# Sums of squares of the head norms as two fp32r matmuls on a split, in place of one fp32 matmul

## The reference, cut to what matters

```
mu = jnp.mean(o, axis=-1, keepdims=True)
var = jnp.mean(jnp.square(o - mu), axis=-1, keepdims=True)
o = (o - mu) * lax.rsqrt(var + EPS)
```

```
o = _rms_norm(o, o_g.astype(f32).reshape(HG_HEADS, HG_DV)).reshape(bsz, seq, HG_WIDTH)
o = o * jax.nn.silu(g_raw.astype(f32))
```

## Time and profile before

| | us |
|---|---|
| median of 3 runs | 3059.87 |
| lowest, highest | 3058.55, 3060.05 |
| the profiled execution's own time | 3058.55 |
| span of its trace | 3056.8 |
| PE busy in the span | 3021.0 (99%) |
| POOL, DVE, ACT busy | 1411.2, 1692.7, 1133.5 |

### The profile page before, as it was taken

The page is one execution under the profiler, slowest core; times in us unless marked ns, Lnnn a source line. Parts: engine busy times, 40 slices in busy tenths (PEclk is TensorE's granted clock), DMA queues, the critical chain, the costliest instruction groups (busy, mean ns, idle before and its releaser), DMA issues.

```text
span 3056.8 us, 41047 instructions
## 1 busy us (share of the span) xinstructions
PE 3021.0 (99%) x13900; PEld 2395.4 (78%) x13900; DVE 1692.7 (55%) x2591; ACT 1133.5 (37%) x1713; POOL 1411.2 (46%) x1040
## 2 busy tenths in 40 slices
PE   8999999999999999999999999999999999999998
PEld 6877777877888887777777788877888888788886
DVE  7974575675434597576577644267772253621214
ACT  4233332364332423233245524236563333422223
POOL 5443443455455453443444555443434444454544
PEclk9999999999999999999999999999999999999999
DMA  4222212212232332222221132221213323232222
GB/s 148 97 69 69 96 69 82 84 42 83 97 102 95 128 99 72 92 75 66 79 90 56 36 131 96 96 97 63 77 68 98 103 83 103 83 103 97 96 96 90
DMA packets 73269, 267.86 MB, mean 88 GB/s; under 512 B 8128, under 2 KB 9024, under 8 KB 72768
## 3 DMA queue, kind: packets, MB, share of 16 engines
q1 hardware_dynamic: 70560, 254.84, 24.9%
q10 hardware_dynamic: 2592, 11.46, 1.0%
HBM read 262.07 MB, written 4.19 MB: 87 GB/s over the span
## 4 chain that ended last, share of the span: by engine, by line
PE 82%; issue 7%; POOL 5%; DVE 3%; DVEq 1%; ACT 0%; POOLq 0%; ACTq 0%
PE gem L356 18%; PE gem L358 18%; PE gem L357 18%; POOL wlo L290 5%; PE xp L500 4%; PE gem L744 2%; PE xp L489 2%; PE gem L746 2%; PE gem L745 2%; PE gem L476 2%; PE gem L477 2%; PE gem L475 2%; PE gem L587 2%; PE gem L610 1%; PE xp L646 1%
## 5 line engine op out<-in xcount | busy, mean ns | idle before, releaser
L290 POOL TENSOR_TENSOR wlo<-raw,whi 128x512 fp32r<-128x512 f32 x956 | 1315.7, 1398 | 1581.2 <-ACT whi L905 1580.9
L905 ACT ACTIVATE whi<-raw 128x1024 fp32r<-128x1024 f32 x478 | 504.6, 1056 | 675.8 <-PE gem L358 466.9
L356 PE MATMUL gem<-zhi,whi 128*128 128x512 f32 x1680 | 666.5, 397 | 0.3 <-DVE zlo L1503 0.3
L358 PE MATMUL gem<-zhi,wlo 128*128 128x512 f32 x1680 | 654.1, 389 | 0.0
L357 PE MATMUL gem<-zlo,whi 128*128 128x512 f32 x1680 | 653.7, 389 | 0.0
L356 PE MATMUL gem<-hhi,whi 128*128 128x512 f32 x1296 | 515.7, 398 | 0.0
L358 PE MATMUL gem<-hhi,wlo 128*128 128x512 f32 x1296 | 504.5, 389 | 0.0
L357 PE MATMUL gem<-hlo,whi 128*128 128x512 f32 x1296 | 504.3, 389 | 0.0
L356 PEld LDWEIGHTS gem<-zhi,whi 128*128 128x128 f32 x1680 | 315.5, 188 | 71.7 <-issue 7.0
L357 PEld LDWEIGHTS gem<-zlo,whi 128*128 128x128 f32 x1680 | 315.5, 188 | 70.7 <-issue 6.5
L358 PEld LDWEIGHTS gem<-zhi,wlo 128*128 128x128 f32 x1680 | 315.4, 188 | 66.0
(11 more groups left out here) (320 smaller groups left out, 3960.3 us busy)
## 6 DMA issues: line engine op xcount, KB each, us to landing
raw<-in_slabs SPq DMA_DIRECT2D x478, 512.0 KB, 3.4
U<-in_x SPq DMA_DIRECT2D x4, 512.0 KB, 7.8
U<-in_x ACTq DMA_DIRECT2D x1, 2048.0 KB, 8.6
xsave<-U ACTq DMA_DIRECT2D x1, 2048.0 KB, 6.5
U<-xsave ACTq DMA_DIRECT2D x1, 2048.0 KB, 8.9
out_y<-yr SPq DMA_DIRECT2D x8, 256.0 KB, 2.1
tab<-in_tab_ret ACTq DMA_DIRECT2D x2, 512.0 KB, 8.1
tab<-in_tab_att ACTq DMA_DIRECT2D x2, 512.0 KB, 3.6
```

The lines of the kernel that those rows point to most:

```text
L290: part = pool.tensor_tensor(wlo[:, k % 4, c], raw[:, k % 2, c], whi[:, k % 4, c].bitcast(f32), O.subtract)
L356: pe.matmul(o, wh, hi, start=(n == 0), stop=False)
L358: mm = pe.matmul(o, wl, hi, start=False, stop=(n == len(terms) - 1))
L905: act.activation(whi[:, k % 4, :], raw[:, k % 2, :], A.Copy).then_inc(hi_done, 1)
```

## The change

The sum over partitions was one fp32 matmul of the squares by fp32 ones. It becomes two fp32r matmuls into the same bank, of the high half and of the low half of the squares, by ones in fp32r. The halves are put into tile 7 of the pair that is free at that time (`zhi`/`zlo` of the layer; in the gating heads the names `Z[DEPTH][0]` on ACT and `zhi` on DVE are the buffer that the order below calls `hhi`). In retention heads DVE makes both halves behind its last add. In gating heads ACT makes the high half behind the square (a third 128x512 instruction, signal `hg_osh`), and DVE makes the low half in `square_rest`, behind the first level of `k_levels`, and signals `hg_osq`. The sum stands three rows later in heads 1 to 6 (25 and 23 for 22 and 20), two rows later in head 0 (29 for 27), and where it was in head 7 (23). ACT makes the fp32r ones once, at the start, and PE's first instruction waits for them too.

```diff
@@ tensor engine @@
             pe.wait_ge(consts, 1)
+            pe.wait_ge(ones_ready, 1)
...
                 def var(hd):
                     pe.wait_ge(ossq, L * 4 + hd + 1)
-                    pe.matmul(xp[:, 1, :], ones[:, :], TT[:, 2, :], start=True, stop=True).then_inc(ovar, 1)
+                    pe.matmul(xp[:, 1, :], ones_r[:, :], zhi[:, 7, :], start=True, stop=False)
+                    pe.matmul(xp[:, 1, :], ones_r[:, :], zlo[:, 7, :], start=False, stop=True)\
+                        .then_inc(ovar, 1)
...
                 pe.wait_ge(hg_osq, p + 1)
-                pe.matmul(xp[:, 2, :], ones[:, :], OSQ, start=True, stop=True).then_inc(hg_var, 1)
+                pe.matmul(xp[:, 2, :], ones_r[:, :], zhi[:, 7, :], start=True, stop=False)
+                pe.matmul(xp[:, 2, :], ones_r[:, :], zlo[:, 7, :], start=False, stop=True).then_inc(hg_var, 1)
                 rows(cuts[4], 32)
 
-            head_products(0, BLOCK_G + 1, BLOCK_U + 1, (14, 16, 18, 23, 27))
-            head_products(1, BLOCK_G + 2, BLOCK_U + 2, (0, 9, 13, 17, 22))
+            head_products(0, BLOCK_G + 1, BLOCK_U + 1, (14, 16, 18, 23, 29))
+            head_products(1, BLOCK_G + 2, BLOCK_U + 2, (0, 9, 13, 17, 25))
             with pe.Fori(2, 7) as p:
-                head_products(p, BLOCK_G + 1 + p, BLOCK_U + 1 + p, (0, 6, 11, 15, 20))
+                head_products(p, BLOCK_G + 1 + p, BLOCK_U + 1 + p, (0, 6, 11, 15, 23))
@@ scalar engine @@
             log_exp()
+            act.wait_ge(consts, 1)
+            act.activation(ones_r[:, :], ones[:, :], A.Copy).then_inc(ones_ready, 1)
             high(0, 0, False)
...
-                act.activation(OSQ, OH, A.Square).then_inc(hg_osq, 1)
+                act.activation(OSQ, OH, A.Square)
+                act.drain()
+                act.activation(Z[DEPTH][0][:, 7, :], OSQ, A.Copy).then_inc(hg_osh, 1)
                 act.wait_ge(hg_var, p + 1)
@@ vector engine @@
-                    tt(TT[:, 2, :], TT[:, 2, :], TT[:, 3, :], O.add).then_inc(ossq, 1)
+                    tt(TT[:, 2, :], TT[:, 2, :], TT[:, 3, :], O.add)
+                    dve.drain()
+                    dve.tensor_copy(zhi[:, 7, :], TT[:, 2, :])
+                    dve.drain()
+                    tt(zlo[:, 7, :], TT[:, 2, :], zhi[:, 7, :].bitcast(f32), O.subtract).then_inc(ossq, 1)
...
                     last = longer(KES[2 * w], KES[w], KF[w])
+                    if w == 16 and p is not None:
+                        square_rest(p)
...
+            def square_rest(p):
+
+                dve.wait_ge(hg_osh, p + 1)
+                tt(zlo[:, 7, :], OSQ, zhi[:, 7, :].bitcast(f32), O.subtract).then_inc(hg_osq, 1)
...
             update(7)
+            square_rest(7)
             head_end(7)
```

More of the change, by code:

```diff
@@ L96, in build @@
         ident = sb("ident", [P, P])
+        ones_r = sb("ones_r", [P, P], f32r)
         ones = sb("ones", [P, P])
@@ L241, in build @@
         hg_osq, hg_var, hg_rstd = sem("hg_osq"), sem("hg_var"), sem("hg_rstd")
+        hg_osh, ones_ready = sem("hg_osh"), sem("ones_ready")
         merged_in, merged_hi = sem("merged_in"), sem("merged_hi")
@@ L2083, in longer, with k_levels @@
                           factor[:, :, None].to_broadcast([P, n, T // n]), O.mult)
-            def k_levels():
+            def k_levels(p=None):
                 dve.tensor_copy(DEC[16], chunks(EB)[:, :, CHUNK16 - 1])
@@ L2157, in _ @@
                 el_k(hd)
-                k_levels()
+                k_levels(p)
                 head_end(p)
```

## The result

The changed kernel takes 3063.46 us (median of 20 runs) where the kernel before takes 3059.61 (20 runs): a ratio of 1.0013 with a 95% interval of 1.0007 to 1.0019. It is slower by 3.9 us. That is within my bound for no change (0.2%, 6.1 us) and within my range, but its sign is clear, and the forecast was +0.3 us: 3.6 us of what happened are not in my sum. One of the changed kernel's 20 runs took 7871 us, a slow one that the ratio leaves out; the others lie between 3062.30 and 3064.80.

The account below looks back on a forecast made before the run. PE was taken to bound the kernel, busy for 3021.0 of 3056.8 us. The terms -3.2 + 0.2 + 0.9 + 1.6 + 1.1 - 0.3 = +0.3 us gave a forecast of 3060.2 us, range 3056.0 to 3063.5.

Parts of the forecast that it names:

- The price of a matmul: At the 16 sums: fp32 matmul 0.85 us, fp32r pair 0.46, saving 0.395 each, at most 6.3 us.
- The retention heads: In the eight retention heads the added DVE work fits into slack, so all savings come through: -3.2 us.
- The start: At kernel start ACT makes the ones before its first copies and shifts all that follows: +0.2 us.
- The place in the gating heads: The later sum delays ACT's root, DVE's chain and the next scores; waits at the scores 7.5 us in all.
- the queue of 7.7 us: Behind the gating root, POOL's four and DVE's five instructions still take 7.7 us, with DVE now going first.
- Rival 1: In gating heads the chain behind the root doesn't hold PE, so the whole saving comes: 3053.8 us; chance 10%.
- its half: No wait at the scores in gating heads 2 to 6 alone, 3.0 us better: 3057.1 us; chance 9%.
- Rival 2: In gating heads POOL delays the low half and PE waits at the sum: up to +8.8 us, 3069; chance 5%.
- rival 3: At the sums, fp32r by a block of ones costs what fp32 did, saving missing: 3066.5 us; chance 4%.
- The step that failed is the sum's last one: Adding the terms for start, retention heads and gating heads over the whole kernel to +0.3 us.
- what a wait leaves behind it: In gating heads 2 to 6 PE waits 0.6 us each and comes out 0.21 later: +1.1 us in all.
- Head 0: In gating head 0 the pair waits 0.05 us and the scores of head 1 come later: +0.9 us.

Follow-up runs that it names:

- run 1: Kernel before with only the retention heads' part and the fp32r ones, gating heads unchanged: 3056.35 us against 3059.72.
- run 3: Kernel before, fp32 matmul kept, only the gating sums moved to 29, 25 and 23 rows from 27, 22 and 20: 3068.75 us against 3059.72.
- run 4: Changed kernel with the gating sums put back to 27, 22 and 20 rows: 3065.48 us against 3059.72 for the kernel before.
- run 5: Changed kernel with the gating sums one row earlier, at 28, 24 and 22 rows: 3060.45 us against 3059.37 for the kernel before.
- run 10: Changed kernel with the sums of gating heads 0 and 1 one row earlier (28 and 24): 3061.49 us against 3059.77 for the kernel before.
- run 12: Changed kernel with nothing altered, profiled a third time to see TensorE's clock: 3062.92 us.
- run 8: Kernel before with nothing altered, profiled once more to see TensorE's clock: 3061.26 us.
- run 2: Kernel before with only the gating heads' part of the change, retention heads unchanged: 3066.28 us against 3059.72.

## Why the prediction was wrong, point by point

The change in the changed kernel's trace, from the same marks in both traces (after minus before, us):

| stretch | forecast | measured |
|---|---|---|
| start | +0.2 | +0.1 |
| 8 retention heads | -3.2 | -3.4 |
| clock, 2040 to 2100 us | 0 | +0.7 |
| gating head 0 up to the scores of head 1 | +0.9 | +1.5 |
| clock behind these scores | 0 | +1.4 |
| head 1 | +1.6 | +1.6 |
| heads 2 to 7 | +0.8 | +1.8 |
| sum | +0.3 | +3.7 |

**The price of a matmul** was right: 0.85 us for the fp32 one, and 0.46 for the pair, so that a retention head is 108.17 us long for 108.59. **The retention heads** were right in sign and size, and run 1 alone gives -3.4 us.

**The start** was right: the first matmul stands at 11.05 us for 10.83, and by row 6 the difference is 0.1.

**The place in the gating heads** was right as a mechanism. The places of the root (0.66 behind the pair for 0.65 forecast), of `head_end` (2.19 for 2.08 behind the pair) and the queue of 7.7 us are those of the working, the waits at the scores are 7.0 us (7.5 forecast): 2.5 in head 1, 1.9 in head 2 (2.0 forecast) and 0.5 in the others (0.6). Run 3 shows that the place alone costs 9.0 us, and run 4 that the pair can't stand at the old one, though one of the three rows can be given back (run 5). Rival 1 is out with its half, as are rivals 2 and 3: PE hardly waits at the sum, and the pair is cheap. (Rival 2's 8.8 us count POOL's full 1.25 us in each of 7 heads; with the slack of 0.6 us that it names, 0.65 and 4.6 us are left.) One reading was wrong: DVE was to go first in the queue, and POOL went first in all seven heads, as before (2295.29, and DVE's L1513 at 2295.33).

**The step that failed is the sum's last one:** "-3.2 + 0.2 + 0.9 + 1.6 + 1.1 - 0.3 = +0.3 us". It put TensorE's clock at nothing, took a wait at its own length, and had head 0 at 0.9 where 1.5 was measured. Of the 3.4 us between the forecast and the trace, 2.1 are the clock (1.4 of them behind the new waits), 1.0 heads 2 to 7 and 0.6 head 0; the start and the retention heads take 0.3 off.

First, **the clock**. I counted on the clock of the kernel before, which was at 2.4 GHz throughout the gating heads. Behind the longer wait of head 1 it fell to 1.2 GHz (PEclk 0.50 over the 3.10 us of the row above), worth 1.4 us in the changed kernel's first profile. Run 10 points to the price in the medians: with the waits of heads 1 and 2 at 1.85 and 1.21 us the time falls by 2.0 us, of which the traces explain 0.4 without the clock (head 1 is 28.20 us from scores to scores, for 28.57 in run 12; head 0 gains nothing, as its wait moved to the sum). The +0.7 earlier in the trace is of the other kind, stretches whose place and length differ from execution to execution (run 8), and isn't shown to be the change's: the wait of 3.0 us has one behind it here, and the one behind the wait of 5.0 us is 3.4 us long for 6.8 before. The Trainium skill, "TensorE: Matmul & The Clock Gate", section "What's actually happening", says that the default is the throttled clock and activity releases it, and that the place at which it changes varies from run to run. The traces agree: the clock fell where PE had stood, and in three profiles of the changed kernel it did so behind head 1, behind both heads and behind head 2. I had not weighed this page in the prediction.

Second, **what a wait leaves behind it**, the term of heads 2 to 6: 0.21 each was forecast, and 0.28 in head 2 and 0.37 to 0.39 in the others were measured. 0.1 of the difference stands where the scores restart: from them to the inter-chunk product are 10.85 us (2273.78 to 2284.63 in head 6) where it was 10.73. The rest is the start of the queue: `head_end` came 0.1 us later behind the root than I took, POOL went first, and the queue ended 1.65 us later against the inter-chunk product, for 1.59 forecast. And in head 7 the wait at the sum ate the saving (4.06 us of difference at its pair, for 3.77 at its scores): -0.3 was forecast, 0 measured.

**Head 0** was forecast at +0.9 and measured at +1.5. DVE there, and PE at the sum:

```profile
2113.04 0.69 DVE L2096 TENSOR_TENSOR U<-U 128x512 f32<-128x512 f32 x1 [0.45 <-issue]
2113.65 0.69 DVE L2162 TENSOR_TENSOR hlo<-U,hhi 128x512 fp32r<-128x512 f32 x1
...
2114.39 0.50 PE L806 MATMUL xp<-hhi,ones_r 128*128 128x512 f32 x1 [0.30 <-DVE hlo L2162]
2114.72 0.39 PE L807 MATMUL xp<-hlo,ones_r 128*128 128x512 f32 x1
```

DVE stood 0.45 us ahead of the first level for nothing that the profile names, where it had stood 0.07 before, and in the loop's later rounds it is 0.17. I had put the pair with 0.05 us of wait; the low half came 0.4 later and PE stood 0.45, restart included. The gap comes with the retention part: it is there in every kernel that has that part, run 1 among them, whose gating heads are those of before, and in none without it. In run 2, the gating part alone, the pair stands where I had put it, 4.86 us behind the inter-chunk product, and the head costs 1.2 (5.26 and 1.5 in the changed kernel). Why DVE instructions that are added in the retention heads make it stays open. The rest of the difference is the root: the pair's second matmul came 0.1 us later behind the first than in the loop (2114.39 to 2114.72), and the queue follows the root through POOL, which starts it, while I took the smaller shift of `head_end`.

In the medians the whole is +3.9, of which the chain makes +1.6 (the table without the clock) and some 2 us are left. That clock stretches make them is shown for single profiles, and run 10 fits it; how often they come over many executions was only inferred from five profiles.

## What to carry to other kernels

When two engines take turns, a result that is moved later on one of them must be followed through everything that stands behind it on the others, up to the next wait of the engine that sets the time; slack there is spent once, and a saving on the leading engine shortens it as well. Try both halves of such a change alone: here one gives 3.4 us (0.1%) and the other takes 6.6, and the retention part alone (3056.35 us) is the fastest version found, faster than both kernels. And price a new wait of TensorE by more than its length when it is long: behind waits of 1.85 to 2.65 us a stretch at half the clock, worth 1.4 to 1.7 us in the traces, followed in seven places of ten here, while in the three kernels whose longest of these waits was 1.78 to 1.85 none did. These runs give no safe length.

## What the runs showed of the hardware that I had not expected

- Behind PE waits of 1.85 to 2.65 us the granted clock fell to 1.2 GHz for over 3 us in seven places of ten, beginning 1.3 us after the restart in the changed kernel's first profile and 0.1 us after it in run 3; in the first it cost 1.4 us. One unchanged wait of 3.0 us was followed by such a stretch in 7 of 14 profiles. Two profiles of one and the same kernel differ by 2.7 us of span with equal waits in the gating heads, 1.4 of it from the start.
- After a wait PE needs about 0.1 us more for the same work: 10.85 us for 10.73.
- In the queue of head 6 DVE's 128x512 instructions took 1.6 to 1.8 us where the last one, alone, took 0.69, and POOL's took 1.72 to 1.74 where its first took 1.30. The nine together took 7.7 us in both kernels, with POOL first in both. This agrees with the exclusive lock of the Trainium skill, "SBUF — State Buffer", section "Who interferes with whom".
- A gap of 0.45 us on DVE in gating head 0 came with DVE instructions added in the retention heads, far ahead of it in time (0.44 in run 1, 0.07 in runs 2 and 3).
